# Mixer of layer 0: gates by function, VectorE a level ahead, latents split into temporary tiles

## The chip, the cores and the metric

The kernel runs on one core of one Trainium2 chip. The metric is device time in microseconds of one execution. Three runs of the kernel before gave 2388.28, 2393.32 and 2398.53 us; the median is 2393.32.

## The reference, cut to what matters

The program is a whole network on 256 latent tokens of width 1024: a first block (self attention, memory attention, gated MLP), then two layers of a second block on 256 latent and 256 context tokens. Everything is float32. The change concerns one part, the mixer of layer 0:

```python
q_g, k_g, v_g, r_g, lr_f, lr_b, c_q, c_kv, k_r = jnp.split(h @ w_in, split_points, axis=-1)
log_gate = lambda lr, wg2, bg: jax.nn.log_sigmoid(lr @ wg2 + bg) / 16      # forward and backward
q  = rms_norm(c_q, q_norm_g) @ w_uq          # 4 heads x (128 plain + 64 rotary)
kv = rms_norm(c_kv, kv_norm_g) @ w_ukv       # 4 heads x (128 key + 128 value)
gla = rms_norm(o_forward + flip(o_backward), gla_norm_g) * jax.nn.silu(r_g)   # gated linear attention
mla = softmax((q . k) * 192 ** -0.5) @ v     # keys: context and latents, with a shared rotary key
y = jnp.concatenate([gla, mla], axis=-1) @ w_out
```

The gated linear attention has 4 heads with 64 key and 128 value channels. Its output at token i sums v_j (q_i . k_j) over the other tokens, each channel decayed by exp of the sum of log gates between j and i.

## The kernel before

**Tiling.** Activations lie feature-major: 128 partitions by 512 columns (256 latents, 256 context tokens) for each of 8 feature tiles. A float32 product is made of three matmuls (`pe_product`, lines 524 to 526) with each operand split into a high and a low fp32r part: high x high, low x high (or high x low), high x low. Weights come in chunks of up to 2048 floats a partition (1 MB) in the order of `plan()`, by DMA from SP into one of three buffers WF. ScalarE casts the high part into WH (line 924), in two halves; VectorE subtracts the low part of the first half (line 1426), GpSimd that of the second (line 2055). WH and WL have two slots each, so a half is cast once the same half of the chunk two places before is read.

**Order.** Five programs (SP, TensorE, VectorE, ScalarE, GpSimd) run side by side, each in the order in which it is written; named events order them (`up` counts a semaphore, `at` gives what to wait for). There is no planner. PSUM banks are taken in a ring (`Banks.take`): `ps` has six, `po` two. To take a bank TensorE waits for the events that its last user named as emptying it.

**The mixer** (`pe_even`, `act_even`, `dve_even`, `pool_even`, one list of steps each). TensorE projects, in this order: gla queries (e_q) with low-rank gates and rotary key (e_lr); gla keys (e_k) with the four gate products (line 817) in the middle; latents c_q and c_kv (e_c, 2 chunks); output gates (e_r, 2); gla values (e_v, 2); then from the normed latents the mla queries (uqn, uqr), keys (ukn) and values (ukv). Into these the *levels* of the gla are strewn, then the mla attention follows (16 units), then the output projection (eout).

**Gates.** log sigmoid(x) = min(x, 0) - ln(1 + exp(-|x|)). ScalarE makes Abs, Exp and Ln in TMP, first for both tiles of the forward direction, then for both of the backward (lines 1217 to 1231). VectorE makes the minimum (1877), the subtraction (1882) and running sums by two scans (1887) into PF. Only then VectorE copies the second key tile out of its bank (1462), and ScalarE the first (960) after its last Ln.

**Levels.** A decay between tokens i and j is written through a common border, in blocks of size B = 1, 2, 4, ... 128, 256, 512: ten levels for each of two pairs of heads, 20 in all. For each, VectorE forms differences of running sums in a slot LV (two slots; lines 1798 to 1807), ScalarE takes Exp (1197), VectorE multiplies by k (1811, 1814) and GpSimd by q (2110, 2113), TensorE multiplies the two (766, 770, 774), and VectorE writes the masked result (1830, 1833) or ScalarE copies it (1183, 1186). The program's item "level h" makes the differences, Exp and products of level h+1 on the three other engines, and the matmuls and masks of level h. Items `gout` (values times the summed matrix, one head; 789 to 793), and `gnorm` (sum of squares, root, scaling; 1838, 1842) follow each ten levels. `gout` takes a `po` bank, which stays taken until line 1838 has read it. 18 items stand between projections; eight are spread over the attention.

**Latents.** CR holds c_q and c_kv. Squares go to TMP (952), their sum over features comes from a matmul with a constant (610), the root is Ln then Exp(-0.5 x) on ScalarE (945, 947), VectorE scales (1441). The high parts go to Hh (1268), the low ones to Hl (1436). Hh and Hl hold the mixer's input until the last projection from it, e_v, is done.

**Attention** (`pe_attention` and its like). Unit i: scores (644) into a `ps` bank, maximum on VectorE (1551), exponential on ScalarE (978), division (1527, 1529), transposition on TensorE (652) two steps later, copy on ScalarE (997), weighing (662) a step later into a `po` bank.

## Time and profile before

| | |
|---|---|
| three runs, median | 2393.32 us (2388.28 to 2398.53) |
| profiled execution | 2393.71 us, span from first to last instruction 2391.9 us |
| mean granted TensorE clock | 0.975 |
| TensorE matmul busy | 2253.3 us (94%) |
| VectorE busy | 1415.8 us (59%) |
| ScalarE busy | 990.7 us (41%) |
| GpSimd busy | 758.9 us (32%) |
| DMA, mean over the span | 138 GB/s |

Busy time is the time in which the engine had an instruction of its kind at work. TensorE's matmuls overlap a little, so their durations add up to more than the busy time. The granted clock is 1 for 2.4 GHz and 0.5 for 1.2 GHz. Span times below are microseconds from the first instruction.

### The profile page before, as it was taken

Reading aid. Unit: us, or ns where it says so; the run is one execution under the profiler, and the core shown is the slowest. Engines: PE = TensorE matmul, PEld = TensorE weight load, DVE = VectorE, ACT = ScalarE, POOL = GpSimd, SP = SyncE. Lnnn points to the kernel's source line nnn. Section 1 sums busy time; section 2 is a strip of 40 time slices with the busy share of each in tenths; the row PEclk is TensorE's granted clock in tenths of the full one; section 3 lists DMA queues with packets and bytes.
Section 4 is the critical chain, followed back from the end, with each engine's and each line's share of the span. In section 5 each row is a group of like instructions: output and inputs, shape, how many; then the busy total and the mean of one; then the engine's idle time right before and its main releaser. Section 6 shows DMA issues by size and latency. Waiting matters only on the chain.

```text
span 2391.9 us, 33198 instructions
## 1 busy us (share of the span) xinstructions
PE 2253.3 (94%) x12738; PEld 1914.2 (80%) x12738; DVE 1415.8 (59%) x2105; ACT 990.7 (41%) x1591; POOL 758.9 (32%) x378
## 2 busy tenths in 40 slices
PE   6999989999999987878899999989999989998997
PEld 6978889978888875755678888878888877778997
DVE  3644544448888566565677766579655463346335
ACT  4555446543223254444452222253223254455443
POOL 3324235442222224421233222234222242214543
PEclk9999999999999998988999999999999989999999
DMA  7427535445554322020224543234454261213553
GB/s 260 153 90 274 218 121 189 162 175 195 182 210 172 111 79 71 29 71 1 97 107 153 182 167 118 97 130 165 178 185 157 99 151 61 71 36 130 178 190 103
DMA packets 79547, 329.93 MB, mean 138 GB/s; under 512 B 18928, under 2 KB 29296, under 8 KB 55840
## 3 DMA queue, kind: packets, MB, share of 16 engines
q1 hardware_dynamic: 79392, 327.81, 39.1%
q8 instruction: 104, 1.70, 0.3%
q14 instruction: 51, 0.42, 0.1%
HBM read 326.70 MB, written 1.08 MB: 137 GB/s over the span
## 4 chain that ended last, share of the span: by engine, by line
PE 82%; DVE 7%; issue 5%; ACT 5%; POOL 1%; DMA 0%; SPq 0%; DVEq 0%; ACTq 0%; POOLq 0%
PE ps L524 25%; PE ps L526 24%; PE ps L525 24%; PE ps L644 3%; PE ps L662 2%; PE ps L652 1%; ACT WH L924 1%; DVE WL L1426 1%; DVE TMP L1502 1%; POOL WL L2055 1%; ACT L947 0%; ACT AR L1197 0%; ACT L945 0%; DVE AR L1798 0%; DVE X L1685 0%
## 5 line engine op out<-in xcount | busy, mean ns | idle before, releaser
L2055 POOL TENSOR_TENSOR WL<-WF,WH 128x1024 fp32r<-128x1024 f32 (+1 forms) x253 | 597.0, 2360 | 1408.9 <-ACT WH L924 1408.4
L524 PE MATMUL ps<-Hh,WH 128*128 128x256 f32 (+1 forms) x2526 | 871.0, 345 | 69.3 <-DVE Hl L1673 28.9
L525 PE MATMUL ps<-Hl,WH 128*128 128x256 f32 (+1 forms) x2526 | 864.2, 342 | 0.0
L526 PE MATMUL ps<-Hh,WL 128*128 128x256 f32 (+1 forms) x2526 | 863.6, 342 | 0.0
L524 PEld LDWEIGHTS ps<-Hh,WH 128*128 128x128 f32 x2526 | 487.4, 193 | 142.7 <-issue 84.5
L924 ACT CAST WH<-WF 128x1024 fp32r<-128x1024 f32 (+1 forms) x508 | 466.4, 955 | 322.5 <-PE ps L526 311.6
L526 PEld LDWEIGHTS ps<-Hh,WL 128*128 128x128 f32 x2526 | 486.6, 193 | 53.5
L525 PEld LDWEIGHTS ps<-Hl,WH 128*128 128x128 f32 x2526 | 487.4, 193 | 52.1 <-issue 0.2
L1502 DVE CUSTOM_DVE_ANT_0 TMP<-AR 128x1024 f32<-128x1024 f32 x216 | 414.6, 1959 | 10.4 <-DMA AR<-in_ada 9.3
L1426 DVE TENSOR_TENSOR WL<-WF,WH 128x1024 fp32r<-128x1024 f32 (+2 forms) x255 | 319.6, 1253 | 150.8 <-ACT WH L924 150.4
L524 PE MATMUL ps<-HIDh,WH 128*128 128x512 f32 (+1 forms) x880 | 307.0, 349 | 3.7 <-DVE WL L1426 3.7
L526 PE MATMUL ps<-HIDh,WL 128*128 128x512 f32 (+1 forms) x880 | 305.0, 347 | 0.0
L525 PE MATMUL ps<-HIDl,WH 128*128 128x512 f32 (+1 forms) x880 | 305.0, 347 | 0.0
L1157 ACT ACTIVATE TMP<-ps 128x512 f32<-128x512 f32 (+1 forms) x88 | 47.8, 543 | 390.4 <-PE ps L526 390.4
L524 PEld LDWEIGHTS ps<-HIDh,WH 128*128 128x128 f32 x880 | 166.6, 189 | 26.5 <-issue 6.2
L525 PEld LDWEIGHTS ps<-HIDl,WH 128*128 128x128 f32 x880 | 166.6, 189 | 21.2 <-issue 0.7
L526 PEld LDWEIGHTS ps<-HIDh,WL 128*128 128x128 f32 x880 | 166.6, 189 | 20.8
L1741 DVE TENSOR_TENSOR TMP<-TMP,ps 128x512 f32<-128x512 f32 (+1 forms) x88 | 54.5, 619 | 188.0 <-PE ps L526 110.9
L1708 DVE SCALAR_TENSOR_TENSOR X<-ps,MOD,X 128x256 f32<-128x256 f32 x136 | 60.3, 479 | 134.0 <-PE ps L526 134.0
L1161 ACT CAST HIDh<-TMP 128x512 fp32r<-128x512 f32 (+1 forms) x88 | 49.9, 567 | 145.1 <-DVE TMP L1741 145.1
L524 PE MATMUL ps<-WH,Hh 128*128 128x256 f32 (+1 forms) x324 | 96.7, 299 | 6.4 <-POOL WL L2055 6.4
L525 PE MATMUL ps<-WL,Hh 128*128 128x256 f32 (+1 forms) x324 | 94.9, 293 | 0.0
(196 smaller groups left out, 2041.0 us busy)
## 6 DMA issues: line engine op xcount, KB each, us to landing
WF<-in_w SPq DMA_DIRECT2D x170, 1024.0 KB, 4.8
AR<-in_ada SPq DMA_DIRECT2D x120, 512.0 KB, 5.7
WF<-in_w SPq DMA_DIRECT2D x80, 704.0 KB, 4.1
AR<-in_piece SPq DMA_DIRECT2D x12, 1024.0 KB, 7.8
AR<-bias_rows SPq DMA_DIRECT2D x3, 1024.0 KB, 14.5
AR<-in_rpb SPq DMA_DIRECT2D x12, 256.0 KB, 6.6
AR<-in_cond SPq DMA_DIRECT2D x2, 1024.0 KB, 6.9
X<-in_x SPq DMA_DIRECT2D x2, 512.0 KB, 4.2
```

What stands on the lines that cost most here:

```text
L524: e.matmul(out, lh, rh, start=first, stop=False)
L525: e.matmul(out, lh, rl, start=False, stop=False)
L526: return e.matmul(out, ll, rh, start=False, stop=end)
L644: m = e.matmul(b[:, c0:c0 + w], a, r, start=n == 0, stop=n == len(pairs) - 1)
L662: m = e.matmul(b[rows, cols], v, pt[:, f:to], start=first, stop=end, skip_group_check=True)
L924: e.copy(h[:, k0:k1, :], src[:, k0:k1, :]).then_inc(*up("w_hi", ("hi", i, q)))
L1161: e.copy(HIDh[:, j, 0:T], t[:, 0:T]).then_inc(*up("hid_hi", (st, "hidh", n)))
L1426: e.tensor_tensor(l[:, k0:k1, :], src[:, k0:k1, :], h[:, k0:k1, :].bitcast(F32), ALU.subtract).then_inc(*up("w_lo", ("lo", i, 0)))
L1502: e.tensor_tensor_reduce(out=WIDE_TMP[r], in0=AW[x % 3], in1=COND[:, r, :], scale=1.0, scalar=0.0, op0=ALU.mult, op1=ALU.add, accum_out=MO ...
L1708: e.scalar_tensor_tensor(out=X[:, j, c], in0=ps[tile][:, c], scalar=MOD[:, l, 8 * g + j, r:r + 1], in1=X[:, j, c], op0=ALU.mult, op1=ALU.a ...
L1741: e.tensor_tensor(t, t, ps[st, "u", n][:, 0:T], ALU.mult).then_inc(*up("gated", (st, "m", n)))
L2055: e.tensor_tensor(l[:, k0:k1, :], src[:, k0:k1, :], h[:, k0:k1, :].bitcast(F32), ALU.subtract).then_inc(*up("p_lo", ("lo", i, 1)))
```

## The change

- `plan()`: the chunks of the mixer come in the order e_c, e_v, uqn, uqr, e_r, ukv; keys and values from c_kv are one chunk of 1024 columns.
- The four gate tiles are handled by function: four Abs, four Exp, then the key tiles are copied (both by ScalarE), then four Ln. The minimum is written into PF directly, subtraction and scans work there in place.
- VectorE's differences are made a level earlier (in item h for level h+2) and its product with k is split off (`dve_keys`).
- The high and low parts of the latents go to `CH_` and `CL_`: `LAT` is laid over ROW and TMP, so they are TMP0 to TMP3, TMP4 to TMP6 and ROW. They are made in the middle of the first v chunk.
- Roots are made in pairs (`act_roots`: all Ln, then all Exp). Heads are handled in pairs (`gouts`, `gnorms`); their products go to `ps` banks and are copied to TMP5 and TMP6, and the squares to SUM and SQ.
- 15 items stand between projections, 9 in the attention. Silu of the output gates moves behind the copies of the mla keys.

```diff
+    CH_ = [LAT_[:, 512 * k + 512:512 * k + 1024] for k in range(4)]
+    CL_ = [LAT_[:, 512 * k:512 * k + 512] for k in (5, 6, 7, 0)]
+    GO = [TMP[5], TMP[6]]
...
+    gla_items = [("level", i) for i in range(10)] + [("gouts", 0)] + [("level", i) for i in range(10, 13)] + [("gnorms", 0)]
+    GLA_FIRST = len(gla_items)
+    gla_items += [("level", i) for i in range(13, 20)] + [("gouts", 1), ("gnorms", 1)]
+    work3 = spread(gla_items[GLA_FIRST:], 16)
+    GATES = [(0, 0), (1, 0), (0, 1), (1, 1)]
 
...
+        def latents():
+            pe_stat(e, "cq", T2, [(TMP[0], ("csum",)), (TMP[2], ("csq", 2))])
+            pe_stat(e, "ckv", T2, [(TMP[3], ("csq", 3))])
+            some(1)
 
         pe_lin(e, CH["e_k"][0], of, T2, [(("gk", j), [("gk", j)]) for j in range(2)], mid=gates)
         for j in range(2):
             pe_lin(e, CH["e_c"][j], of, T2, [(("c", c), [("c", c)]) for c in (2 * j, 2 * j + 1)], mid=one_gla)
-            if j == 0:
-                some(1)
         some(1)
-        pe_stat(e, "cq", T2, [(TMP[0], ("csum",)), (TMP[2], ("csq", 2))])
-        pe_stat(e, "ckv", T2, [(TMP[3], ("csq", 3))])
+        for i in range(2):
+            pe_lin_t(e, CH["e_v"][i], of, [(("gv", i, t), [("gv", i, t)]) for t in range(4)], mid=one_gla if i else latents)
+            some(1)
+        aq = [(CH_[k], CL_[k], [("ch", k), ("cl", k)]) for k in range(4)]
+        pe_lin(e, CH["uqn"][0], aq[0:3], T2, [(("qn", j), [("qn", j)]) for j in range(4)], fresh=True)
+        some(1)
+        pe_lin(e, CH["uqr"][0], aq[0:3], T2, [(("qr", j), [("qr", j), ("qrc", j)]) for j in range(2)])
         some(1)
         for j in range(2):
             pe_lin(e, CH["e_r"][j], of, T2, [(("gr", c), [("gr", c)]) for c in (2 * j, 2 * j + 1)], mid=one_gla)
             some(1)
-        for i in range(2):
-            pe_lin_t(e, CH["e_v"][i], of, [(("gv", i, t), [("gv", i, t)]) for t in range(4)], mid=one_gla)
-            if i == 0:
-                some(1)
-        some(2)
-        aq = acts(hf, "ch", "cl")
-        pe_lin(e, CH["uqn"][0], aq[0:3], T2, [(("qn", j), [("qn", j)]) for j in range(4)], fresh=True)
...
+    def act_roots(e, *norms):
+
+        for name, n, which, after in norms:
+            e.wait_ge(*at(("stat", name)))
+            for x in after:
+                e.wait_ge(*at(x))
+            e.activation(STAT[which], ps["stat", name], ACT.Ln, scale=D / n, bias=eps).then_inc(*up("ln", ("ln", name)))
+        for name, _, which, _ in norms:
+            e.wait_ge(*at(("ln", name)))
+            e.activation(STAT[which], STAT[which], ACT.Exp, scale=-0.5).then_inc(*up("root", ("root", name)))
+
...
+        elif what == "gouts":
+            for g in (2 * h, 2 * h + 1):
+                e.wait_ge(*at(("go", g)))
+                for x in [("gnd", g - 2), ("stat", ("g", g - 2))] if h else [("end", CH["uqr"][0]), ("mix0", "res", KT - 1)]:
+                    e.wait_ge(*at(x))
+                e.copy(GO[g % 2], ps["go", g]).then_inc(*up("a_evict", ("gox", g)))
+                e.activation([SUM, SQ][g % 2], ps["go", g], ACT.Square).then_inc(*up("square", ("gsq", g), ("gn", g)))
+        elif what == "gnorms":
+            act_roots(e, *[(("g", g), P, g % 2, [("gt", g - 2)] if h else [("qr", g % 2)]) for g in (2 * h, 2 * h + 1)])
 
...
+        for i, (d, n) in enumerate(GATES):
+            e.wait_ge(*at(("gate", d, n)))
+            e.activation(TMP[i], ps["gate", d, n], ACT.Abs, bias=vec("bg_b" if d else "bg_f", n)).then_inc(*up("decay", ("gabs", d, n)))
+        for i, (d, n) in enumerate(GATES):
+            e.wait_ge(*at(("gabs", d, n)))
+            e.activation(TMP[i], TMP[i], ACT.Exp, scale=-1.0).then_inc(*up("decay", ("gexp", d, n)))
         act_splits(e, CH["e_k"][0])
-        act_evict(e, GK[:, 0, :], ("gk", 0)).then_inc(*up("a_evict", ("gk", 0)))
-        act_decays(e, 0)
+        for j in range(2):
+            act_evict(e, GK[:, j, :], ("gk", j)).then_inc(*up("a_evict", ("gk", j)))
+        for i, (d, n) in enumerate(GATES):
+            e.wait_ge(*at(("gexp", d, n)))
+            e.activation(TMP[i], TMP[i], ACT.Ln, bias=one).then_inc(*up("decay", ("gln", d, n)))
...
+            if h + 2 < len(GLA):
+                dve_decays(e, h + 2)
+        elif what == "gnorms":
+            for g in (2 * h, 2 * h + 1):
+                e.wait_ge(*at(("root", ("g", g))))
+                e.wait_ge(*at(("gox", g)))
+                e.scalar_tensor_tensor(out=GO[g % 2], in0=GO[g % 2], scalar=vec("gla_g"), in1=STAT[g % 2], op0=ALU.mult,
+                                       op1=ALU.mult).then_inc(*up("scaled", ("gt", g)))
+            for g in (2 * h, 2 * h + 1):
+                e.wait_ge(*at(("gt", g)))
+                e.wait_ge(*at(("grs", g)))
+                e.tensor_tensor(GR[:, g, :], GO[g % 2], GR[:, g, :], ALU.mult).then_inc(*up("gla_out", ("gnd", g)))
 
...
+        for d, n in GATES:
+            e.wait_ge(*at(("gabs", d, n)))
+            e.tensor_scalar(PF[:, d, n, :, 1:257], ps["gate", d, n].rearrange("p (s t) -> p s t", s=2), vec("bg_b" if d else "bg_f", n),
+                            0.0, ALU.add, ALU.min).then_inc(*up("gate_min", ("gmin", d, n)))
         dve_splits(e, CH["e_k"][0])
-        dve_evict(e, GK[:, 1, :], ("gk", 1))
-        dve_decays(e, 0)
+        for i, (d, n) in enumerate(GATES):
+            e.wait_ge(*at(("gln", d, n)))
+            e.wait_ge(*at(("gmin", d, n)))
+            e.tensor_tensor(PF[:, d, n, :, 1:257], PF[:, d, n, :, 1:257], TMP[i].rearrange("p (s t) -> p s t", s=2),
+                            ALU.subtract).then_inc(*up("gate_sub", ("gsub", d, n)))
+            for s in range(2):
+                e.memset(PF[:, d, n, s, 0:1], 0.0)
+            e.wait_ge(*at(("gsub", d, n)))
+            for s in range(2):
+                m = e.tensor_tensor_scan(PF[:, d, n, s, 1:257], view(one, 0, [0, S]), PF[:, d, n, s, 1:257], 0.0, ALU.mult, ALU.add)
+            m.then_inc(*up("scan", ("pf", d, n)))
+            if i == 1:
+                dve_decays(e, 1)
...
+            if i == 0:
+                for k in range(4):
+                    dve_scaled(e, CR[:, k, :], CR[:, k, :], vec("q_g", k) if k < 3 else vec("kv_g"), STAT[k // 3], ("cs", k), ("csq", k),
+                               ("root", "cq" if k < 3 else "ckv"))
+                for k in range(4):
+                    dve_low(e, CL_[k], CR[:, k, :], CH_[k], ("ch", k), ("cl", k))
+            some(1)
```

## Rows read from the trace of the kernel before

**Rows 1.** The page, part 1: busy us of each engine, share, instructions.
```profile
PE 2253.3 (94%) x12738; PEld 1914.2 (80%) x12738; DVE 1415.8 (59%) x2105; ACT 990.7 (41%) x1591; POOL 758.9 (32%) x378
```

**Rows 2.** Windows: stretch, length, busy us (instructions) by engine, PEclk, DMA share, GB/s.
```profile
905.65:912.70 7.05, 7.05 (x25) 5.39 (x24) 4.77 (x13) 5.59 (x8) 0.00 (x0) 0.80 0.18 76
912.70:923.30 10.60, 0.02 (x2) 0.04 (x1) 7.86 (x14) 8.10 (x10) 3.66 (x2) 0.62 0.00 0
923.30:1073.79 150.49, 131.25 (x765) 103.66 (x765) 86.24 (x141) 65.66 (x91) 51.42 (x27) 0.92 0.16 54
1073.79:1141.50 67.71, 55.77 (x289) 37.58 (x290) 35.15 (x97) 32.70 (x71) 7.13 (x4) 0.89 0.00 1
```

**Rows 3.** Waits of TensorE, 895 to 1142: waiting line, releaser, total us, times, longest.
```profile
PE ps L524 <- issue: 10.6, 1, 10.6
PE ps L766 <- POOL AR L2110: 7.5, 6, 4.4
PE ps L662 <- issue: 4.7, 2, 2.3
PE ps L789 <- DVE TMP L1838: 3.6, 1, 3.6
PE ps L524 <- DVE Hl L1436: 3.3, 1, 3.3
PE ps L524 <- DVE AR L1855: 3.3, 1, 3.3
PE ps L662 <- DVE TMP L1838: 2.8, 1, 2.8
PE ps L652 <- DVE TMP L1529: 2.0, 2, 1.3
...
PE ps L817 <- issue: 1.1, 1, 1.1
```

**Rows 4.** Timeline of ScalarE, gate stage: start, us, line, operation [idle before].
```profile
906.67 1.28 ACT L1231 ACT_TABLE_LOAD   x1
...
917.11 0.56 ACT L960 COPY AR<-ps 128x512 f32<-128x512 f32 x1
...
919.58 1.28 ACT L1197 ACT_TABLE_LOAD   x1
```

**Rows 5.** Timeline of VectorE, gate stage.
```profile
917.34 1.27 DVE L1887 TENSOR_TENSOR_SCAN AR<-CST,TMP 128x256 f32<-128x256 f32 x2
...
919.24 3.37 DVE L1887 TENSOR_TENSOR_SCAN AR<-CST,TMP 128x256 f32<-128x256 f32 x2
922.53 0.66 DVE L1462 COPY AR<-ps 128x512 f32<-128x512 f32 x1
```

**Rows 6.** Timeline of GpSimd: a split, and a product with q.
```profile
919.64 2.42 POOL L2055 TENSOR_TENSOR WL<-WF,WH 128x1024 fp32r<-128x1024 f32 x1 [14.26 <-ACT WH L924]
...
956.57 1.78 POOL L2110 TENSOR_TENSOR AR<-AR 128x512 f32<-128x512 f32 x1 [2.12 <-ACT AR L1197]
```

**Rows 7.** Windows: half a chunk of matmuls; beside a wait of 1.0; after 4.4.
```profile
932.69:938.36 5.67, 5.67 (x26) 4.43 (x24) 1.29 (x2) 0.57 (x1) 0.00 (x0) 1.00 0.00 0
954.00:957.00 3.00, 2.45 (x6) 1.06 (x6) 1.88 (x4) 1.55 (x2) 0.88 (x2) 1.00 0.00 0
969.00:972.00 3.00, 2.42 (x18) 2.10 (x19) 3.00 (x4) 0.55 (x1) 2.90 (x2) 0.65 0.02 5
```

**Rows 8.** Waits of VectorE and of ScalarE, 895 to 1142.
```profile
DVE AR L1811 <- ACT AR L1197: 18.0, 16, 1.1
...
ACT AR L1197 <- DVE AR L1801: 53.3, 16, 5.9
```

**Rows 9.** Groups of VectorE by form, 895 to 1072: xcount, busy us, mean ns.
```profile
L1798 DVE TENSOR_TENSOR AR<-AR 128x256 f32<-128x256 f32 x13 | 14.1, 1084 | 0.0
L1426 DVE TENSOR_TENSOR WL<-WF,WH 128x1024 fp32r<-128x1024 f32 x8 | 10.6, 1323 | 22.0 <-ACT WH L924 22.0
...
L1800 DVE TENSOR_TENSOR AR<-AR 128x256 f32<-128x256 f32 x13 | 5.4, 416 | 0.0
```

More of the change, by code:

```diff
@@ L147, in plan @@
             wide("e_c", "even", 512, 1568)
-            wide("e_r", "even", 512, 1024)
             wide("e_v", "even", 512, 512)
@@ L152, in plan @@
             out.append(("uqr", k3, [("uq", np.concatenate([eo(192 * h + 128) for h in range(4)]))]))
-            out.append(("ukn", [0], [("ukv", np.concatenate([rng(256 * h, 128) for h in range(4)]))]))
-            out.append(("ukv", [0], [("ukv", np.concatenate([rng(256 * h + 128, 128) for h in range(4)]))]))
+            wide("e_r", "even", 512, 1024)
+            out.append(("ukv", [0], [("ukv", np.concatenate([rng(256 * h + 128 * v, 128) for v in range(2) for h in range(4)]))]))
             for c in range(4):
@@ L259, in program @@
     MOD = sb("MOD", 2 * 72 * 2)[:, :].rearrange("p (l n r) -> p l n r", l=2, r=2)
+    with nc.sbuf_tensor("LAT", [P, 8 * 512], F32R) as LAT_:
+        pass
     ROW = sb("ROW", 512)[:, :]
@@ L1279, in act_even @@
         some(1)
-        act_splits(e, CH["ukn"][0])
+        for j in range(2):
+            act_splits(e, CH["e_r"][j])
+            some(1)
+            for c in (2 * j, 2 * j + 1):
+                act_evict(e, GR[:, c, :], ("gr", c)).then_inc(*up("a_evict", ("gr", c)))
+            some(1)
+        act_splits(e, CH["ukv"][0])
         for j in (0, 2):
@@ L1283, in act_even @@
         some(1)
-        act_splits(e, CH["ukv"][0])
+        act_silus(e)
+        for c in range(4):
+            e.wait_ge(*at(("gr", c)))
+            e.activation(GR[:, c, :], GR[:, c, :], ACT.Silu).then_inc(*up("silu", ("grs", c)))
         for t in range(4):
@@ L1919, in dve_even @@
         for j in range(2):
-            dve_rotate(e, QR[:, j, :], P, ps["qr", j], ("qr", j), TMP[2 * j], TMP[2 * j + 1], ("qrrot", j), ("qr", j))
+            dve_rotate(e, QR[:, j, :], P, ps["qr", j], ("qr", j), STAT[j][:, 0:S], STAT[j][:, S:T2], ("qrrot", j), ("qr", j))
         some(1)
-        dve_splits(e, CH["ukn"][0])
+        for j in range(2):
+            dve_splits(e, CH["e_r"][j])
+            some(2)
+        dve_splits(e, CH["ukv"][0])
         for j in (1, 3):
             dve_evict(e, KN[:, j, :], ("kn", j))
-        some(1)
-        dve_splits(e, CH["ukv"][0])
-        some(1)
+        some(2)
         def end(e, hr, b):
@@ L2143, in pool_even @@
         e.tensor_tensor(TMP[0], TMP[0], TMP[1], ALU.add).then_inc(*up("p_sum", ("csum",)))
-        some(2)
+        some(1)
+        for i in range(2):
+            chunk(CH["e_v"][i])
+            some(2)
+        for name in ("uqn", "uqr"):
+            chunk(CH[name][0])
+            some(1)
         for j in range(2):
@@ L2147, in pool_even @@
             some(2)
-        for i in range(2):
-            chunk(CH["e_v"][i])
-            some(2 - i)
+        chunk(CH["ukv"][0])
         some(2)
-        for name in ("uqn", "uqr", "ukn", "ukv"):
-            chunk(CH[name][0])
-            some(1)
         for items in work3:
```

187 lines of the change are left out of this document (57 added, 130 removed).

## The prediction

> **What bounds the kernel now.** The page's first part comes first: TensorE is busy 94% of the span and VectorE, the next, 59% [rows 1], so time can only come out of TensorE's waits, its clock or its work. The stretches come second. The change touches layer 0's mixer, which TensorE goes through from 905.65 to 1141.50; nothing before or behind is edited. The 235.85 us split into the second half of the key projection (7.05), a hole without matmuls (10.60), projections and gate levels up to the first transposition of the attention (150.49) and the attention (67.71) [rows 2]. TensorE's waits are third: the groups shown sum to 38.9 us, 1.1 of it ahead of 905.65; what is smaller is counted as work that stays [rows 3]. The clock is fourth: mean granted 0.80, 0.92 and 0.89 in the three working stretches [rows 2]. Taken as shares of the 1.2 and 2.4 GHz levels, 7.05 x 0.20 + 150.49 x 0.08 + 67.71 x 0.11 = 20.9 us at most are lost to the low one. The sum is made against the profiled execution's own 2393.7 (span 2391.9 and 1.8 around it), 0.4 above the median shown, so nothing is corrected. Floor: 2393.7 - 38.9 - 20.9 = 2334.
>
> **Part 1, the gate stage.** The hole of 10.6 has no visible releaser [rows 3]. The code tells it: the next projection (e_c) takes two PSUM banks that key tiles gk0 and gk1 hold. ScalarE copies gk0 at 917.11, after twelve gate functions and three table loads; VectorE copies gk1 at 922.53, after all scans [rows 4, 5]. In the new order ScalarE copies both ahead of its Ln pass, and the eight functions before that (about 0.6 each, like the copy's 0.56 [rows 4]) take the 5 us of gate products and key projection. The hole becomes one copy (0.56) and a handover, 0.8: **-9.8**. The gate product that waited 1.1 for the bank of "lr" (held until VectorE's copy krd) now waits only for a ScalarE copy done some 3 us earlier: **-1.1**. Minimum, subtraction and scans stay as many; they write PF instead of TMP, the same 128x512. Two of four table loads of this stage (1.28; first and last [rows 4]) go, in time that no longer holds TensorE.
>
> What is late next is the low half of e_c's second chunk, which VectorE makes behind the scans. From the key copies: a load 1.28 and an Ln 0.7, then four times a subtraction (0.66, as the copy at 922.53) and a pair of scans, 1.27 [rows 5], 7.7; the differences of level 1, which the new order puts among them, 4 x 0.42 less overlap, 1.4; the split 1.3 [rows 9]: 12.4. GpSimd's own split falls into it: the pair of scans beside it took 3.37 instead of 1.27 [rows 5, 6], +2.1. Together 14.5. TensorE meanwhile has the first e_c chunk, two halves of 5.67 [rows 7], and level 0, 1.1: 12.4. With 0.9 for the residual multiply beside it: **+3.0** (bounds 0 and 5.5, if a second lock of 2.5 falls in).
>
> **Part 2, the levels.** Each level is a chain in one place: VectorE forms differences (four operations), ScalarE takes Exp, VectorE multiplies k while GpSimd multiplies q, TensorE starts. ScalarE stood 53.3 us for the differences in 16 waits, VectorE 18.0 for Exp [rows 8], TensorE 7.5 for q [rows 3]. With the differences a level ahead Exp finds its data ready and q follows GpSimd's split at once. The longest of the six waits, 4.4, stood behind two roots, which load four tables in a row; now they load two, with half a chunk of v behind them on TensorE. **-7.0** of 7.5.
>
> VectorE pays in density. A level costs it about 3.3: differences 1.4, one product and two masked copies of about 0.65 each. Two levels, split 1.3, eviction 0.7 and about 3.3 lost to GpSimd (the first difference has a mean of 1.08, the third 0.42 [rows 9]) are 12 us in a chunk of 13.5 (4 halves' worth of matmul and two levels). In the first v chunk scaling and low parts of the latents come on top, eight operations like the copy of 0.66: 16, against 16.5. No wait follows by this count, but hardly any slack stays. I expect c1's bank before level 1 (1.0; VectorE's copy stands behind the differences), k of level 5 (0.3), the low half of e_r (0.5), and 2.5 at handovers where the count leaves under 1 us: **+4.3** (bounds 0 and 15, three quarters of a microsecond at each of 20 levels).
>
> By the Trainium skill, page "SBUF — State Buffer", section "Who interferes with whom", a VectorE instruction with two SBUF inputs and a GpSimd instruction that reads SBUF exclude each other for the whole instruction. The rows agree for splits, 2.1 us; none shows q's product beside differences, since the old order hardly lets them meet. The rule speaks against this change, and the second rival is what it would do here.
>
> **Part 3, latents to TMP and ROW.** The copies no longer wait for the last v product, nor uqn for its low parts: **-3.3** (L1436). The other 3.3 (L1855) is a bank held by the rotation of the queries. It moves: 5 us of rotation now run beside the first half (5.67) of e_r, ahead of level 9. But ScalarE's Exp of level 9 stands behind two copies that wait for the rotation, and q's product (1.8 [rows 6]) behind that: 2.4 remain, **-0.9**. Merged ukv: one DMA and one split fewer, the same 24 products. The bank of kn1 is copied by VectorE behind the split of the first output chunk, and mv's second product needs it: **+1.4** (bounds 0 and 3). The moved DMAs stay three chunks ahead of use on SP, at a DMA share of 0.16 [rows 2]: 0, and if one were late, its 4 us less the 13 of a chunk still 0.
>
> **Part 4, heads and attention.** go moves to the six ordinary banks and is copied at once, so the wait of 3.6 for gn (L789) ends: **-3.6**. The weighing's 4.7 in two waits (L662, issue) are ScalarE copies behind an Exp that waited for differences: **-4.7**. One level more follows the first transposition and one fewer precedes it: 0. The pair of roots at the end costs ScalarE 5.2 (two loads, four functions of 0.66) instead of 3.9, so the last 2.8 stay: 0. At the attention's start gnorms of heads 0 and 1 (roots, then four VectorE operations) stand before the first maximum, as ScalarE's roots before the first Exp: TensorE's 2.0 (L652) become about 4: **+2.0** (bounds -1 and 6).
>
> By the Trainium skill, page "ScalarE: Activation LUTs", section "Table sets: the hidden batching unit", one set holds both exp and ln, so alternating them costs one load. The trace disagrees: four loads of 1.28 in the gate stage, at each change in either direction [rows 4]. By the rule gathering would save no load, and some 2.6 of the 7.0 in part 2 would stay.
>
> **Sum.** Waits: -9.8 - 1.1 + 3.0 - 7.0 + 4.3 - 3.3 - 0.9 + 1.4 - 3.6 - 4.7 + 2.0 = -19.7. Clock: full (1.00) beside waits of 1.0 in 954 to 957, but 0.65 after the one of 4.4 [rows 7]. The loss is as if some 12 spells had cost 1.7 each. Five stay: at the gates, the second e_c chunk, level 9, the attention's start and its end; 8.9, so **-12.0**. Together -31.7: **2362**.
>
> **Rivals.**
> (a) *Only the hole goes.* The levels' waits move from GpSimd to VectorE, nearly full in the v chunks. Then the gate stage gives -7.9, the heads -3.6, the clock two spells, 3.4: -15, 2379. For it: the count of 16 against 16.5. Against: 53.3 us of ScalarE waiting show how long the chain idled.
> (b) *The lock.* Each q product (1.8 [rows 6]) blocks differences: 13 levels before the attention, 23 us on VectorE. It is busy 86.24 of 150.49 there [rows 2]; in some 127 us that leaves 17, unevenly spread, and about 9 come through: 2371.
> (c) *No new waits*: -19.7 less their 10.7, and two spells of clock kept (-17.5): -48, 2346. For it: none of the new waits is seen, all are worked out.
> (d) *Slower: the clock.* A few long waits are traded for many short ones and TensorE stays at 1.2 GHz. Work at full clock is 235.9 - 37.8 - 20.9 = 177; with 19 us of waits left it breaks even at a mean granted clock of 177 / 217 = 0.82 while busy (177 / 198 = 0.89 now). At 0.77 the mixer takes 230 + 19 = 249, +13: 2407. Against: the full clock beside waits of 1.0.
> That the change doesn't do what it says: if the hole had another cause (the chunk's low half, say), it would stay, with its clock: 2374, counted in (b), which it resembles in time.
>
> **Chances.** Forecast 0.50, (a) 0.17, (b) 0.18, (c) 0.11, (d) 0.04; the forecast's own range is 2355 to 2369. The range 2349 to 2381 leaves out most of (c), a third of (a), and (d). Half a per cent, about what a measurement of this kernel can tell from no change, is 12 us, so 2381: faster is the forecast, (b), (c) and two thirds of (a), 0.90; same 0.06; slower 0.04.
>
> **What would show it.** e_c follows the key projection within 1.5 us (wrong if 5 or more remain). Its second chunk waits 1 to 5 us for WL from VectorE. No Exp of a level waits over 1 us for differences after the first two. Before uqn there is no wait, before level 9 about 2.4, around the attention's first transposition 3 to 5, before the last heads' products none. ScalarE loads 8 tables less. (b) shows as first differences with means of 1.5 us and more; (d) as a mean clock in the mixer below 0.89. The forecast is wrong if the mixer shortens by less than 24 or more than 39 us, or if a stretch outside it changes by over 2.

## The result, and the profile after

Before took 2393.81 us in the median (2388.28 to 2398.53, four runs), after 2363.81 (2363.2 to 2366.29, four): a ratio of 0.9877, 95% interval 0.9855 to 0.99. Forecast was 2362 with a range of 2349 to 2381. The profiled execution of after took 2366.29, its span is 2364.5; that of before is given above.

The page of after, part 1, against [rows 1]; TensorE has the same 12738 instructions and is busy 7.1 us less:

```profile
PE 2246.2 (95%) x12738; PEld 1912.7 (81%) x12738; DVE 1422.6 (60%) x2103; ACT 982.0 (42%) x1587; POOL 753.2 (32%) x378
```

The windows of after, against [rows 2]: start of the mixer to the beginning of the key projection's second half, that half with what is left of the hole behind it (0.7), projections and levels up to the attention's first transposition, the attention. Columns are length, then busy us (instructions) by engine, granted clock, DMA share, GB/s.

```profile
879.48:908.01 28.53, 28.53 (x107) 21.56 (x108) 20.27 (x27) 20.19 (x33) 9.13 (x5) 0.91 0.14 45
908.01:913.81 5.80, 5.08 (x24) 3.87 (x22) 2.26 (x4) 3.46 (x8) 0.65 (x1) 1.00 0.35 144
913.81:1052.70 138.89, 122.62 (x733) 98.20 (x733) 96.51 (x150) 66.63 (x95) 49.17 (x26) 0.95 0.17 58
1052.70:1113.30 60.60, 55.53 (x321) 38.98 (x322) 43.25 (x106) 32.06 (x73) 7.60 (x6) 0.92 0.00 1
```

The same windows of before, its first stretch and their sum; its mixer is 265.05 us with TensorE busy 222.23:

```profile
876.11:905.65 29.54, 28.48 (x105) 21.02 (x105) 20.38 (x27) 18.86 (x32) 9.75 (x5) 0.90 0.16 54
...
sum 265.05, PE 222.23 PEld 167.35 DVE 154.40 ACT 130.90 POOL 71.96; mean PE 44.45 PEld 33.47 DVE 30.88 ACT 26.18 POOL 14.39
```

After's mixer ends where the first matmul of the output projection starts, 1112.99: 233.5 us, TensorE busy some 211.5. So the mixer is **31.5 us shorter**: 20.8 of idle time (42.8 to 22.0) and 10.7 of busy time, which for the same matmuls is the clock. The rest of the span differs by some 4 us the other way: ahead of the mixer after takes 879.5 us and before 876.1, with 827.7 and 824.8 us of busy time for the same matmuls. The same kernel, profiled again, took 875.3 there and had the same mixer (233.6) in a span of 2360.5, so that part is drift.

TensorE's waits in the mixer of after, against [rows 3]: waiting line, releaser, total us, times, longest.

```profile
PE ps L525 <- DVE WL L1441: 8.3, 2, 7.3
PE ps L653 <- DVE TMP L1544: 4.0, 4, 2.8
PE ps L663 <- issue: 3.1, 1, 3.1
PE ps L525 <- DVE HAh L1477: 2.9, 1, 2.9
PE ps L775 <- POOL AR L2128: 2.1, 1, 2.1
PE ps L525 <- ACT AR L972: 0.7, 1, 0.7
...
PE ps L767 <- POOL AR L2125: 0.3, 1, 0.3
```

The hole is the 0.7. The six waits for q are one of 0.3, gn's wait (L789) and both of 2.3 in the weighing are gone. What took their place is led by a wait of 7.3 for WL, the low half of the second e_c chunk, where 3.0 was forecast.

VectorE's timeline ahead of that wait shows why (start, us, line, operation, the idle time before in brackets). TensorE wanted the split of line 1441 at 926.25:

```profile
919.77 2.44 DVE L1813 TENSOR_TENSOR AR<-AR 128x256 f32<-128x256 f32 x1
922.13 1.51 DVE L1814 TENSOR_TENSOR AR<-AR 128x256 f32<-128x256 f32 x1
923.57 0.41 DVE L1815 TENSOR_TENSOR AR<-AR 128x256 f32<-128x256 f32 x1
...
924.95 2.36 DVE L1908 TENSOR_TENSOR_SCAN AR<-CST,AR 128x256 f32<-128x256 f32 x2
...
927.93 3.37 DVE L1908 TENSOR_TENSOR_SCAN AR<-CST,AR 128x256 f32<-128x256 f32 x2
931.23 2.21 DVE L1441 TENSOR_TENSOR WL<-WF,WH 128x1024 fp32r<-128x1024 f32 x1
```

GpSimd's timeline in the same stretch:

```profile
919.55 2.38 POOL L2070 TENSOR_TENSOR WL<-WF,WH 128x1024 fp32r<-128x1024 f32 x1 [10.89 <-ACT WH L936]
921.88 1.49 POOL L2083 TENSOR_TENSOR X<-X,SQ 128x512 f32<-128x512 f32 x1
925.49 1.28 POOL L2125 TENSOR_TENSOR AR<-AR 128x512 f32<-128x512 f32 x1 [2.13 <-ACT AR L1224]
928.16 2.60 POOL L2070 TENSOR_TENSOR WL<-WF,WH 128x1024 fp32r<-128x1024 f32 x1 [1.39 <-ACT WH L936]
930.72 1.64 POOL L2083 TENSOR_TENSOR X<-X,SQ 128x512 f32<-128x512 f32 x1
```

Each of the five GpSimd instructions falls on one of VectorE, which ends behind it by no more than its own usual length: 2.44 and 1.51 for a difference of 0.41, 2.36 and 3.37 for a pair of scans of 1.27, 2.21 for a split of 1.20. The excess is 2.0 + 1.1 + 1.1 + 2.1 + 1.0 = 7.3 us, and the wait is as long. The forecast had counted one such meeting with a split (2.1) and 0.9 for a residual multiplication. Not every VectorE instruction is held: the four minima of the gates, which read PSUM, began at 907.54 beside a residual multiplication that ended at 908.66 and took 2.73 us for four, their usual 0.7 each.

### The profile page after: what moved, and what is told of

Same layout as the page of the kernel before. It is cut to its first block, busy times and chain, and to the rows that moved or that the text cites. A ratio compares the mean times of both kernels' runs of the same rounds, so it can differ in the third digit from the quotient of the medians.

```text
span 2364.5 us, 33183 instructions
## 1 busy us (share of the span) xinstructions
PE 2246.2 (95%) x12738; PEld 1912.7 (81%) x12738; DVE 1422.6 (60%) x2103; ACT 982.0 (42%) x1587; POOL 753.2 (32%) x378
## 3 DMA queue, kind: packets, MB, share of 16 engines
HBM read 326.70 MB, written 1.08 MB: 139 GB/s over the span
## 4 chain that ended last, share of the span: by engine, by line
PE 84%; DVE 6%; issue 5%; ACT 4%; POOL 1%; DMA 0%; DVEq 0%; SPq 0%; ACTq 0%; POOLq 0%
PE ps L525 26%; PE ps L526 25%; PE ps L527 25%; PE ps L645 2%; PE ps L663 2%; PE ps L653 1%; ACT WH L936 1%; DVE WL L1441 1%; POOL WL L2070 1%; DVE TMP L1517 0%; DVE AR L1854 0%; DVE X L1700 0%; ACT L959 0%; DMA WF<-in_w 0%; DVE TMP L1544 0%
## 5 line engine op out<-in xcount | busy, mean ns | idle before, releaser
L2070 POOL TENSOR_TENSOR WL<-WF,WH 128x1024 fp32r<-128x1024 f32 (+2 forms) x253 | 594.9, 2352 | 1385.3 <-ACT WH L936 1384.8
L525 PE MATMUL ps<-Hh,WH 128*128 128x512 f32 (+1 forms) x2504 | 860.3, 344 | 62.0 <-DVE Hl L1688 28.9
L526 PE MATMUL ps<-Hl,WH 128*128 128x512 f32 (+1 forms) x2504 | 854.3, 341 | 0.0
L527 PE MATMUL ps<-Hh,WL 128*128 128x512 f32 (+1 forms) x2504 | 853.5, 341 | 0.0
L936 ACT CAST WH<-WF 128x1024 fp32r<-128x1024 f32 (+3 forms) x507 | 466.2, 956 | 322.3 <-PE ps L527 312.3
L525 PEld LDWEIGHTS ps<-Hh,WH 128*128 128x128 f32 x2504 | 482.3, 193 | 133.6 <-issue 79.3
L525 PEld LDWEIGHTS ps<-HIDh,WH 128*128 128x128 f32 x880 | 167.1, 190 | 26.7 <-issue 6.3
L525 PE MATMUL ps<-WH,Hh 128*128 128x256 f32 x320 | 94.3, 295 | 6.4 <-POOL WL L2070 6.4
L1758 DVE TENSOR_TENSOR HIDl<-TMP,HIDh 128x512 fp32r<-128x512 f32 (+1 forms) x88 | 59.4, 675 | 55.7 <-ACT HIDh L1173 55.7
```

Source lines behind the costliest of these rows:

```text
L525: e.matmul(out, lh, rh, start=first, stop=False)
L526: e.matmul(out, lh, rl, start=False, stop=False)
L527: return e.matmul(out, ll, rh, start=False, stop=end)
L936: e.copy(h[:, k0:k1, :], src[:, k0:k1, :]).then_inc(*up("w_hi", ("hi", i, q)))
L1758: e.tensor_tensor(HIDl[:, j, 0:T], t, HIDh[:, j, 0:T].bitcast(F32), ALU.subtract).then_inc(*up("hid_lo", (st, "hidl", n)))
L2070: e.tensor_tensor(l[:, k0:k1, :], src[:, k0:k1, :], h[:, k0:k1, :].bitcast(F32), ALU.subtract).then_inc(*up("p_lo", ("lo", i, 1)))
```

## Experiments

All compute the whole reference. Every kernel's ratio is to the kernel before, run beside it on the same chip. "Mixer" is from the first e_q matmul to the first one of the output projection, in the profiled execution; "idle" is the part of it without matmuls. Before has 265.1 with 42.8 idle, after 233.5 with 22.0.

| kernel | median us | ratio (95%) | mixer | idle |
|---|---|---|---|---|
| after, again | 2365.76 | 0.9878 (0.9863 to 0.9892) | 233.6 | 22.1 |
| gates alone | 2388.67 | 0.9969 (0.9958 to 0.9981) | 257.4 | 36.9 |
| own level | 2370.71 | 0.9893 (0.9877 to 0.9909) | 240.8 | 26.7 |
| split first | 2361.35 | 0.9859 (0.9843 to 0.9874) | 232.2 | 23.2 |
| residual later | 2358.26 | 0.9843 (0.9827 to 0.9858) | 231.7 | 21.5 |
| pair put off | 2358.28 | 0.9845 (0.9829 to 0.986) | 227.9 | 17.1 |
| four places | 2365.57 | 0.9876 (0.9857 to 0.9895) | 232.0 | 22.5 |
| one table set | 2356.43 | 0.9845 (0.983 to 0.9859) | 223.9 | 15.9 |
| one set, everywhere | 2345.56 | 0.9785 (0.9771 to 0.9799) | 224.9 | 13.4 |
| before, one set | 2383.27 | 0.9943 (0.993 to 0.9956) | 248.9 | 29.9 |
| joined | 2338.53 | 0.9756 (0.9742 to 0.977) | 218.8 | 12.0 |

> The kernel after once more, unchanged, beside the next three on one chip: its time should lie at 0.986 to 0.989 of before; how far its mixer (233.5) and the stretch behind it (1251) move by themselves is the measure for the small differences of the others.

It did: 0.9878, mixer 233.6, every wait within 0.1 of after's. The rest of a span can be compared only to some 4 us. The mixer moves less, but not by tenths alone: one table set and one set, everywhere run the same mixer instructions and differ by 1.0 (223.9 and 224.9), with idle time of 15.9 and 13.4 and busy time of 208.0 and 211.5. So a gain of 1 or 2 us in the mixer that the waits do not show is not shown to be one. The medians move more: residual later is 7.5 us faster than after, again, on another chip, with a mixer only 1.9 shorter. The readings below rest on the waits.

**Gates alone.** Before, with the gate stage of after on all engines:

```
-                (CH["e_lr"][0], T2, [(("lr", 0), [("lrt",), ("krd",)])]))
+                (CH["e_lr"][0], T2, [(("lr", 0), [("lrt",), ("krrot",), ("krc",)])]))
...
         act_splits(e, CH["e_k"][0])
+        for j in range(2):
+            act_evict(e, GK[:, j, :], ("gk", j)).then_inc(*up("a_evict", ("gk", j)))
+        for i, (d, n) in enumerate(GATES):
...
```

> The kernel before with the gate stage of the kernel after alone (four Abs, four Exp, both key copies, four Ln; minimum and scans in PF; the lr bank freed by ScalarE), levels, latents, heads untouched. Theory (the hole is the price of the key copies' place, the rest of the 31.6 us comes from the look-ahead, the latents and the heads): the hole of 10.6 becomes 1 or less, the second e_c chunk waits 5 to 7 for its low half instead (no differences of level 1 ahead of it, so 1.4 less than the 7.3 of after), the waits for GpSimd's q (7.5), for gn (3.6) and before the last weighing (4.7) stay. The mixer goes from 265.4 to 252 to 258, the time to about 2384. Rival 1 (the gates carry nearly all of it, since the levels were hidden): mixer 236 to 242, time 2368. Rival 2 (the hole has another cause, for example the next chunk's weights): it stays, mixer 264, time 2392.

The mixer is 7.6 us shorter, as the theory has it, and the hole is 0.7. The price of the new order does not appear at the second e_c chunk, where 5 to 7 was expected, but at level 1 (5.8), which in the old order stands ahead of that chunk and covers its split; the waits for q rise from 7.5 to 12.0:

```profile
PE ps L768 <- POOL AR L2100: 12.0, 5, 5.8
...
PE ps L791 <- DVE TMP L1834: 3.6, 1, 3.6
```

So of the 9.9 us that the hole gives, some 6 come back in the same stage, as 7.3 do in after. By the mixers, three quarters of the change's 31.5 us are not the gates.

**Own level.** After, with the look-ahead undone:

```
+                dve_decays(e, h + 1)
                 dve_keys(e, h + 1)
...
-            if h + 2 < len(GLA):
-                dve_decays(e, h + 2)
...
-            if i == 1:
-                dve_decays(e, 1)
```

> The kernel after with the differences of a level again formed with that level's keys, directly ahead of its Exp, no level ahead (and none among the scans). Theory (the look-ahead hides the chain differences, Exp, q): ScalarE's wait for differences goes back from 16.5 to 40 us or more, TensorE waits 5 to 9 us more for GpSimd's q products, and the second e_c chunk waits 1.4 to 2.4 less; the mixer is 4 to 8 us longer than 233.8, time about 2370. Rival (look-ahead is worth nothing, the gains are the gates, banks and latents): mixer 231 to 234, time 2361 to 2364.

The mixer is 7.3 longer than after's, 4.7 of it idle time; the time is 0.15% longer, which the intervals do not tell apart. The waits do:

```profile
PE ps L767 <- POOL AR L2122: 5.1, 4, 1.9
PE ps L663 <- ACT TMP L1009: 4.9, 4, 1.4
PE ps L653 <- DVE TMP L1544: 4.6, 1, 4.6
PE ps L775 <- POOL AR L2125: 3.4, 1, 3.4
```

The waits for q return by 6.1 (L767 5.1 for 0.3, L775, which is level 9, 3.4 for 2.1) and new ones appear in the attention, while the second e_c chunk waits 1.6 instead of 7.3. ScalarE waits 51.0 us for differences, after 16.5. Of the 5.7 that the chunk gives back only 1.4 is the work of the differences; the rest is that one pair of scans was held (4.39 for 1.27, an excess of 3.1) instead of five instructions (7.3): the last scans and the split came before GpSimd's second split, as in the residual run below.

**Split first.** After, one instruction moved:

```
             if i == 1:
+                dve_splits(e, CH["e_c"][0])
                 dve_decays(e, 1)
...
-            dve_splits(e, CH["e_c"][j])
+            if j:
+                dve_splits(e, CH["e_c"][j])
```

> The kernel after with VectorE making the low half of the second e_c chunk behind the first two scans, ahead of the differences of level 1 and the other two gates; same instructions, one moved. Theory (the wait of 7.3 us is only VectorE's queue ahead of the split: three blocks of scans and differences, lengthened 7.3 us in five places where GpSimd reads SBUF at the same time): the wait falls below 1, the keys of level 1 come at the same time as now (about 934), so level 1 waits 2 to 3 for them; TensorE gets 4 to 5 us back, the mixer becomes 228 to 231, time 2359. Rival (weights or the high half come late): the second e_c chunk still waits 5 or more, mixer 233 to 236. Rival 2 (VectorE is full, the wait only moves): level 1 or 2 wait as much, 7 us, mixer 234.

The wait only moved, as the second rival has it, though not for its reason (pair put off shows that VectorE was not full). The wait for WL is gone, and one of 5.7 stands at level 1 for the PSUM bank that VectorE's copy of c1 (L1477) frees; the attention's transpositions wait 6.0 for 4.0. TensorE's idle time is 1.1 us more than in after, so the 1.3 by which the mixer is shorter comes from busy time and says nothing of the order:

```profile
PE ps L767 <- DVE AR L1477: 5.7, 1, 5.7
```

The keys of level 1 came at 933.17, where the theory had them; it had overlooked that the copy of c1 stands behind them, at 936.29.

**Residual later.** After, GpSimd's order alone:

```
             pool_splits(e, i)
+            if i in CH["e_c"]:
+                return
```

> The kernel after with GpSimd's two multiplications of the residual behind the splits of the two e_c chunks put off (they follow in later chunks, so the last is made one output-gate chunk later); same instructions, GpSimd order alone. Theory (a VectorE instruction with two SBUF inputs stands still while GpSimd reads SBUF): two of the five places in which VectorE is held between 919 and 933 go, the wait of the second e_c chunk falls from 7.3 to 4.8 to 6.2; mixer 1 to 2.5 shorter. Rival (VectorE's scans are long by themselves, 3.4 us is their length): the wait stays within 0.3 of 7.3 and the scans' durations stay.

The chunk waits 3.1 instead of 7.3, more than the two meetings taken away (2.1): everything behind came 2 us earlier, so the second pair of scans and the split passed ahead of GpSimd's split, which met a product with k instead. VectorE, to be held against the timeline of after above:

```profile
922.68 0.41 DVE L1814 TENSOR_TENSOR AR<-AR 128x256 f32<-128x256 f32 x1
...
924.40 2.37 DVE L1908 TENSOR_TENSOR_SCAN AR<-CST,AR 128x256 f32<-128x256 f32 x2
...
927.39 1.27 DVE L1908 TENSOR_TENSOR_SCAN AR<-CST,AR 128x256 f32<-128x256 f32 x2
928.58 1.20 DVE L1441 TENSOR_TENSOR WL<-WF,WH 128x1024 fp32r<-128x1024 f32 x1
929.70 2.88 DVE L1832 TENSOR_TENSOR AR<-AR 128x512 f32<-128x512 f32 x1
```

and GpSimd:

```profile
920.10 2.38 POOL L2070 TENSOR_TENSOR WL<-WF,WH 128x1024 fp32r<-128x1024 f32 x1 [12.47 <-ACT WH L936]
924.94 1.28 POOL L2125 TENSOR_TENSOR AR<-AR 128x512 f32<-128x512 f32 x1 [2.46 <-ACT AR L1224]
928.71 3.32 POOL L2070 TENSOR_TENSOR WL<-WF,WH 128x1024 fp32r<-128x1024 f32 x1 [2.49 <-ACT WH L936]
```

The difference of 1.51 is 0.41, the scans of 3.37 are 1.27, the split of 2.21 is 1.20. The rival, that the scans are long by themselves, is out. The holding goes both ways: GpSimd's split, issued while VectorE's ran, takes 3.32 instead of 2.4, and the product with k behind it 2.88 instead of 0.7. TensorE's idle time falls by 0.6 only, not by the 4.2 of this wait: those for the attention's transpositions grew from 4.0 to 5.8, that of the e_r chunk from 1.0 to 2.0.

**Pair put off.** After, VectorE's queue in the order below (gate(i) is one subtraction with its scans):

```
+        gate(0)
+        gate(1)
+        dve_splits(e, CH["e_c"][0])
+        dve_decays(e, 1)
+        some(1)
+        dve_evict(e, CR[:, 1, :], ("c", 1))
+        gate(2)
+        gate(3)
+        dve_splits(e, CH["e_c"][1])
```

> The kernel after with VectorE's order in the gate stage changed once more: low half of the second e_c chunk behind the first two scans, then differences and keys of level 1, copies of level 0, copy of tile c1, and only then the two gates of the second head pair (used from level 9 on). Theory (in the run with the split alone moved, the copy of c1 stood behind those two gates, and TensorE waited 5.7 for it at level 1; VectorE has room later, where it idled 4 us): neither the second e_c chunk nor level 1 waits over 1.5 us, the mixer is 5 to 8 us shorter than 233.5. Rival (VectorE is simply full up to the first v chunk, so the work put off makes level 2, the v chunk's low half or the squares of the latents late): waits of 5 or more appear between 938 and 960, mixer within 2 of 233.5.

The mixer is 5.6 shorter than after's, 4.9 of it idle time. Between 915 and 960 one wait is left, 2.1 for the copy of c1, over the 1.5 expected, where GpSimd's next split again held the differences ahead of it (2.61 and 1.48). So the 7.3 was a matter of order and of the lock, not of a full VectorE.

**Four places.** After, kn0 to kn2 copied by ScalarE; Exp of level 9 ahead of the rotation's copies; VectorE's scaling of heads 0 and 1 in the attention's second step and that of heads 2 and 3 behind its last; the last two transposed tiles copied by VectorE.

```
-        for j in (0, 2):
+        for j in (0, 1, 2):
             act_evict(e, KN[:, j, :], ("kn", j))...
...
         act_splits(e, CH["uqr"][0])
+        some(1)
...
+        work = [[("gnorms", 0)] + x if i == 1 else x ...]
...
+            if name == "mla" and 14 <= i - 2 < n:
...
+                e.tensor_copy(TMP[3 + (i - 2) % 2][:, 0:w], ps[name, "t", i - 2][:, 0:w])...
```

> The kernel after with four places undone where one engine's order kept TensorE waiting, no work less: tiles kn0 to kn2 copied by ScalarE and kn3 by VectorE ahead of its split; ScalarE's Exp of level 9 ahead of the two copies that wait for the rotation; VectorE's scaling of the first two heads behind the first maximum of the attention instead of ahead; the last two transposed tiles copied by VectorE, since ScalarE stands in two roots there. Theory (each wait is the order of one queue, as the steps of the prediction say): mv's second product waits under 1 (2.9), level 9 under 0.5 (2.1), the first transposition under 1 (2.8), the last weighing under 1 (3.1), the first low half of the heads for the output perhaps 1 more; waits -8 to -10, mixer 222 to 227. Rival (the engines behind are full, so each wait moves to the next step): mixer within 3 of 233.5.

A miss: TensorE's idle time is 22.5 for 22.0, and the 1.6 us of the mixer are busy time. Two of the four did what they should (mv 2.9 to 0.4, level 9 2.1 to none), and the first transposition waits under 1 instead of 2.8. But what was moved now made others wait:

```profile
PE ps L767 <- DVE AR L1859: 3.7, 2, 3.5
PE ps L663 <- DVE TMP L1583: 3.4, 1, 3.4
PE ps L653 <- DVE TMP L1544: 2.5, 4, 0.8
PE ps L611 <- DVE AR L1859: 2.5, 1, 2.5
...
PE ps L525 <- DVE HAh L1477: 0.4, 1, 0.4
```

The scaling (3.4 us on VectorE) now stood ahead of the keys of level 13, which waited 3.5; the last copy on VectorE (3.4) stood behind a low part that waits for ScalarE's cast, and ScalarE was in the same two roots as before. The 2.5 is a bank that level 12's copies free, behind VectorE's split of the first output chunk.

**One table set.** After, and one set asked for by hand:

```
+        e.preload_act_table_set("natural_log_exp_and_others")
         e.wait_ge(*at(("mix0l", KT - 1)))
...
             e.activation(GR[:, c, :], GR[:, c, :], ACT.Silu)...
+        e.preload_act_table_set("natural_log_exp_and_others")
```

> The kernel after with ScalarE's table set that holds both exp and ln loaded by hand once ahead of the gates and once behind the Silus, in place of the loads that the compiler puts at each change: six loads of 1.28 us fewer in the mixer, the same functions. If one set serves both (the Trainium skill, page ScalarE: Activation LUTs, section Table sets: the hidden batching unit), no load stands between Ln and Exp; theory for the time: only the loads in front of the last weighing lie on the path, its wait of 3.1 falls by 2.5, level waits behind the latents' roots were none, the start of the attention gains 0 to 1: mixer 229 to 232. The second e_c chunk may wait up to 1.3 less, as the Ln pass starts a load earlier. Rival (loads are all hidden): mixer within 1.5 of 233.5. Rival 2 (the set is loaded again at each change all the same): ten loads as before.

More than expected: 9.6 us, 6.1 of it idle time. The mixer has three loads instead of nine, and from the Ln of the gates to the Exp of level 1 ScalarE has none:

```profile
913.84 2.56 ACT L1256 ACTIVATE TMP<-TMP,CST 128x512 f32<-128x512 f32 x4
916.30 1.98 ACT L936 CAST WH<-WF 128x1024 fp32r<-128x1024 f32 x2
923.15 1.06 ACT L1224 ACTIVATE AR<-AR 128x1024 f32<-128x1024 f32 x1 [4.87 <-DVE AR L1818]
```

The waits:

```profile
PE ps L525 <- DVE WL L1443: 3.7, 2, 2.8
PE ps L653 <- DVE TMP L1546: 3.3, 4, 1.8
...
PE ps L663 <- issue: 0.8, 1, 0.8
```

The last weighing waits 0.8 for 3.1 and the attention's start 1.8 for 2.8, as expected. The second e_c chunk waits 2.8 for 7.3, where a load of 1.3 was expected: as in the residual run the earlier scans (the last pair 1.27, not 3.37) slipped ahead of GpSimd's split. A small shift decides how many instructions meet.

**One set, everywhere.** As before, and the set also in the function with which the kernel loads ln at nine other places:

```
     def act_logs(e):
-        e.preload_act_table_set("natural_log")
+        e.preload_act_table_set("natural_log_exp_and_others")
```

> The kernel after with the set that holds exp and ln loaded by hand in the mixer, as in the run before, and also in the nine other places where the kernel loads the ln set by hand. Theory: the mixer stays at 224 (223.9 with the mixer alone), and each layer norm, where TensorE waits for the first low half (five waits of up to 6.1, three of up to 5.4), has its Ln and Exp follow at once: -1.28 in each of eight places, outside -8 to -11, time 2346 to 2350. Rival (the load lay beside the variance on other engines, so it is hidden): outside within 2, time 2356.

The time is 20 us below after's. The mixer is 1.0 longer than in the run before (224.9), outside it 2115.8 of span are left, 11 less than with after, again (2126.9). The five waits for the first low half of a stage (line 1688 of after, 1690 here) show it, 28.9 us in after and here

```profile
PE ps L525 <- DVE Hl L1690: 23.4, 5, 5.1
```

that is 1.1 each, close to one load of 1.28. The three others (line 1451 of after, 1453 here), for which the same was expected, hardly changed: 8.3 for 8.7 in after, again. So of the 11 us the five waits show 5.5; the rest lies in smaller waits and in drift.

**Before, one set.** The same two lines in the kernel before.

> The kernel before, its order untouched, with the set that holds exp and ln loaded by hand once ahead of the gates and once behind the Silus; 17 loads in the mixer become 3 or 4. It tells how much of the change's 31.8 us was a price of table loads that one line removes as well. Theory (the hole was twelve functions, three loads and the scans ahead of the key copies): the hole shrinks by two to three loads, 10.6 to 7 or 8; the longest wait for q (4.4, behind two roots of four loads) falls below 2; the waits of 3.6 and 4.7 fall by 1.3 each; the mixer is 8 to 12 shorter than 265.3, time 2383 to 2386. Rival (VectorE's differences, not the loads, set the levels, and the scans set the hole): mixer 262 to 265.

The mixer is 16.1 us shorter against 8 to 12 expected, 12.9 of it idle time, with three loads instead of 17. The hole is 2.7 where 7 or 8 was expected, the waits for q 4.5:

```profile
PE ps L766 <- POOL AR L2112: 4.5, 5, 2.0
...
PE ps L524 <- issue: 2.7, 1, 2.7
```

From the mixer's start to the first e_c matmul it takes 40.7 us, before 47.2, after 34.3. Of these 6.5 us less, 3.8 are three loads that stood ahead of VectorE's copy of the second key tile, and 2.1 the last pair of scans, 1.27 now and 3.37 before, since GpSimd's split starts behind it (922.02). So half of the 12.9 us that after gains up to the first e_c matmul could be had by those two lines; the whole change on top of them is worth 25.0 (248.9 to 223.9).

**Joined.** The order of the pair put off, with the copy of c1 also ahead of the differences of level 2; residual later; Exp of level 9 and the copies of kn as in four places, with VectorE's split of the first output chunk behind level 12; the scaling of the first heads directly behind the first maximum; the one set everywhere. New against those:

```
+        dve_gla(e, *gi.pop(0), between=lambda: dve_evict(e, CR[:, 1, :], ("c", 1)))
...
+        dve_evict(e, KN[:, 3, :], ("kn", 3))
+        some(1)
         dve_splits(e, CH["ukv"][0])
...
+        work = [[("gnorms", 0)] + x if i == 0 else x ...]
```

> A version that joins what paid: VectorE's order in the gate stage as in the run that put the second head pair off, with the copy of c1 also ahead of the differences of level 2; residual multiplications behind the e_c splits put off; Exp of level 9 ahead of the rotation's copies; kn0 to kn2 on ScalarE, kn3 on VectorE, and VectorE's split of the first output chunk behind level 12 (in the run before, the wait of mv had come back as 2.5 behind that split); scaling of the first heads directly behind the first maximum; the table set with exp and ln by hand, in the mixer and in all other places where ln is loaded. Theory (the waits are orders of queues and add up): in the mixer no wait over 1.5 us, sum of waits under 9 (22 in after), mixer 213 to 220 (233.6); outside, each norm's chain is one load of 1.28 shorter where TensorE waits, eight or nine places, -6 to -12; time 2333 to 2345. Rival (VectorE is full, waits reappear behind each other): mixer 222 to 228, time 2345 to 2352.

2338.53 us, 2.4% below before and 1.2% below after; mixer 218.8, as expected. TensorE's waits in it:

```profile
PE ps L653 <- DVE TMP L1546: 3.4, 4, 1.3
PE ps L645 <- ACT HAl L972: 2.0, 1, 2.0
PE ps L525 <- DVE WL L1443: 2.0, 1, 2.0
```

with 4.5 more in seven groups below 1: 11.9, not under 9, and two waits of 2.0 are over the 1.5 expected. Outside the mixer it gains 7.4 us on after, again, where one set, everywhere gained 11; the difference is within what spans drift.

## Why the prediction was right, and where it was not

The time is 2 us and the mixer 0.2 us from the forecast (31.5 for 31.7), and so is its division: idle time -20.8 for -19.7, clock -10.7 for -12.0. That the total fits to 0.2 us is luck: inside it errors of +4.3 and +1.5 stand against -2.8 and -3.6. Term by term, forecast first:

- The hole: -9.8, was -9.9 (10.6 to 0.7). The cause read from the code (key copies behind functions and scans) was right; gates alone shows it.
- The bank of "lr": -1.1, gone.
- The second e_c chunk: **+3.0, was +7.3**. The queue ahead of the split was listed rightly; the failed step is "GpSimd's own split falls into it: +2.1", one meeting, and 0.9 for the residual. There were five. Even the upper bound, 5.5 with a second lock, was too low. Residual later and one table set show the lock as the cause, and pair put off the remedy.
- Waits for q: -7.0, was -7.2; own level brings 4.8 of it back, and 1.3 more at level 9.
- Small new waits: **+4.3, was +1.5** (0.95 at e_r, 0.5 at a bank). Handovers of 2.5, taken from the count of 16 against 16.5, did not appear. (Where that working says "4 halves' worth of matmul" its 13.5 us are two halves, 11.3, and two levels.)
- uqn -3.3 and level 9 -0.9: gone, and 2.1 left for 2.4 expected. Exp of level 9 behind the rotation was the cause: moved ahead, the wait ended.
- mv: **+1.4, was +2.9**, within its bounds. VectorE's copies stood not only behind the split but behind a difference that GpSimd's split of the same chunk (1032.99, 2.58 us) held for 2.62.
- gn -3.6 and the weighing -4.7: both gone. The end: 0, was +0.3; the start of the attention: +2.0, was +2.0.
- Not in the forecast: 3.6 us in small waits for copies of levels and for stat products, which it had counted as work that stays, went.
- The clock: -12.0, was -10.7. The step, 1.7 us for each spell of waiting that ends, was not tested, and busy time moves by 3.5 between two runs of the same mixer instructions; so this agreement says little.

The hole and the look-ahead have runs of their own (gates alone, own level). The latents in TMP and ROW, the heads in pairs and the new order of the chunks have none by themselves: that they took away the waits of 3.3, 3.6 and 4.7 is read from these waits being gone.

The rivals: VectorE is busy 96.5 of 138.9 us in the long stretch, before 86.2 of 150.5, so (a) had a case, but the levels' waits did not move to VectorE. (b), the lock, struck in the gate stage and hardly more than before in the levels. By form, 12 differences each in after,

```profile
L1814 DVE TENSOR_TENSOR AR<-AR 128x256 f32<-128x256 f32 x12 | 11.6, 966 | 0.0
L1813 DVE TENSOR_TENSOR AR<-AR 128x256 f32<-128x256 f32 x12 | 10.8, 901 | 0.1
L1815 DVE TENSOR_TENSOR AR<-AR 128x256 f32<-128x256 f32 x12 | 6.0, 504 | 0.0
```

the first was to have a mean of 1.5 and more under (b) and has 0.90, before 1.08 [rows 9]; other operations of the level take the blow, the second (0.97, before 0.75) and the product with k (0.88, before 0.69). Added up over the levels between gate stage and attention, what differences, products with k and splits take beyond their undisturbed length is some 15 us in after and 13 in before, not 23 more. (c) is out: the second e_c chunk, mv and the attention's start wait where they did not. (d) found no support: the clock in the long stretch is 0.95, before 0.92. The forecast said that no Exp waits over 1 us for differences after the first two; two do, 1.27 and 2.69; no level waited for either. Eight table loads fewer, as said: 17 to nine. One of its own signs of being wrong did show, a stretch outside the mixer that changes by over 2: the one ahead of it is 3.4 longer. The second profile of after is 0.8 shorter there than before's, so this was drift, and the bound of 2 was too narrow.

On the table sets the prediction let the trace overrule a rule too early. It read from four loads in a row that sets with exp and ln are separate. The Trainium skill, page "ScalarE: Activation LUTs", section "Table sets: the hidden batching unit", says that one set holds both; the run with that set shows no load between Ln and Exp. What the trace had shown was the choice that is made where none is written. The forecast's time is unharmed, since after has the loads, but the cheapest gain of the case lay there.

## What to carry to other kernels

A split or a scan on VectorE that TensorE waits for has to be laid where GpSimd is idle, or first in the queue: count every GpSimd instruction that reads SBUF in that stretch, each of which, in these traces, holds a VectorE instruction with two SBUF inputs for up to its own length. When a wait is undone by moving one instruction, read what now stands behind it, bank copies above all. And where exp and ln alternate, ask for the set with both by name before reordering anything.

## What the hardware showed that was not expected

- A VectorE instruction with two SBUF inputs and a GpSimd instruction that reads SBUF exclude each other, in both directions: a difference of 0.41 us took 2.44 beside a GpSimd split of 2.38, and that split 3.32 when VectorE's was ahead of it. The Trainium skill says so (page "SBUF — State Buffer", section "Who interferes with whom"), and the traces agree; what was new is how sensitive the sum is: two meetings of 2.1 us in all were taken away, the scans came 2 us earlier, and 4.2 us of wait went.
- A table load costs 1.28 us on ScalarE, but on before 14 fewer loads (17.9 us) shortened the mixer by 16.1, 12.9 of it TensorE's idle time: though ScalarE is busy only 41% of the span, most of them lay in chains that TensorE waits for. Not all of the gain is the loads' own length; 2.1 of it is a meeting with GpSimd that no longer took place.
- The clock went with the idle time, but loosely: from before to after 20.8 us less of it came with 10.7 us less for the same matmuls (0.92 to 0.95 and 0.89 to 0.92 granted in the two long stretches), in the joined kernel 10.0 less with 4.7 less (0.98 granted over its mixer), but one set, everywhere, with 13.4 idle, needs as long for them as after (211.5) with 22.0.
